# One load instead of two for the gate/up weights of each expert, begun after the second half of the products

## The chip, the cores and the metric

The kernel runs on one core of a Trainium2 chip. The metric is the device time of one execution in microseconds (us). The kernel before takes 1398.07 us, the median of three runs (1396.43, 1398.07 and 1402.14 us).

## What is computed

One transformer layer in float32 for 512 tokens of width 1024: a mixer of four kinds of attention, a layer norm, then a mixture of experts and a second layer norm. The change lies in the mixture of experts alone:

```python
def swiglu(x, w_gate, w_up, w_down):
    return (jax.nn.silu(x @ w_gate) * (x @ w_up)) @ w_down

def step(acc, blk):                      # a block of up to 128 tokens of one expert
    tok, w, e = blk
    yb = swiglu(x_pad[tok], w_gate_e[e], w_up_e[e], w_down_e[e]).astype(jnp.float32) * w[:, None]
    return acc.at[tok].add(yb), None
```

There are 64 experts (and a shared one). The gate and up matrices of an expert are 1024x256 each, together 2 MB; its down matrix is 256x1024, 1 MB. Each token goes to 8 experts.

## The kernel before, in words

The attention part ends some 560 us after the start. The router and the shared expert follow, and the loop over the 64 experts, one block of 128 rows each, runs from about 684 to 1330 us. This loop is what the change touches.

The weights of an expert come in three transfers of 1 MB, all issued by SyncE (queue SP): `load_first` (L537) and `load_second` (L540) bring the two halves of the gate/up weights, 8 KB a partition each, and `load_down` (L543) the down weights. They land in `raw[b]`, b = e % 2, so there are two buffers. ScalarE copies each third into `w_hi_e` with reduced mantissa (L1109), and VectorE writes the rest, raw minus high, into `w_lo_e` (L1426). `w_lo_e[b]` lies at the same addresses as `raw[b]`: a piece of the buffer is free for the next load only when TensorE has finished the products that read the low part.

TensorE works through expert e in this order, called A, turn, B and D below:

- A(e): `gate_up(e, 0)`, 12 products of the first half (L838 high x high, L841 high x low, L844 low x high), which then increments `gu_a`;
- turn: `turn_h(e-1)` (L856) and `turn_slots(e+1)` (L910), transposes;
- B(e): `gate_up(e, 1)`, the same lines for the second half, which increments `gu_b`;
- D(e-1): `down(e-1)`, 12 products (L891), which increments `y_done`.

SP issues the first half of expert e when A(e-2) is done, the second half when B(e-2) is done, and the down weights of e-1 when D(e-3) is done. The four shared tiles count in the same semaphores, hence the `e + QT - 1` of the waits.

ScalarE handles its instructions strictly in this order for expert e: copy out the result of e-2 (`out_y`, L1141), `high_first(e+1)`, `copy_hT(e-1)` (L1127), `high_x(e+1)` (L1133), `high_second(e+1)`, the silu of e (L1123), `high_down(e)`. So `copy_hT(e-1)`, which D(e-1) needs, stands behind `high_first(e+1)`, which waits for the first half of the weights of e+1. VectorE follows with `low_down(e-1)`, the low part of hT (L1447), `low_first(e+1)`, the low part of x (L1452), `make_h(e)` (L1441) and `low_second(e+1)`. GpSimd scatters the results (L1642) and gathers the rows (L1637) with indirect DMAs in a queue of its own, q0; all of SP's transfers are in q1.

Of the kernel before, what the change touches and what calls it, by code (L numbers as in the profile page):

```python
# [37 lines left out]
QT = SEQ // P  # L38
# [20 lines left out]
GU = KT * 2 * F  # L59
# [121 lines left out]
def build(nc, a, out):  # L181
# [9 lines left out]
    with ctx:  # L191
# [3 lines left out]
        def sem(name):  # L195
            return ctx.enter_context(nc.semaphore(name))
# [104 lines left out]
        raw, w_lo_e, w_hi_e = [None, None], [None, None], [None, None]  # L301
# [110 lines left out]
        p0_in = [sem(f"p0_in{b}") for b in range(2)]  # L412
        p1_in = [sem(f"p1_in{b}") for b in range(2)]
        dn_in = [sem(f"dn_in{b}") for b in range(2)]
        p0_hi = sem("p0_hi")
        p1_hi = sem("p1_hi")
# [10 lines left out]
        gu_a = sem("gu_a")  # L427
# [31 lines left out]
        def _(sp):  # L459
# [70 lines left out]
            PART = GU // 2  # L530
# [2 lines left out]
            sp.dma_start(raw[1][:, PART:GU], a["w_gu_s"][:, PART:GU]).then_inc(p1_in[1], 16)  # L533
            sp.dma_start(down_of(raw[1]), a["w_down_s"][0].rearrange("(t p) n -> p t n", p=P)).then_inc(dn_in[1], 16)

            def load_first(e):
                sp.dma_start(raw[e % 2][:, 0:PART], a["w_gu"][e][:, 0:PART]).then_inc(p0_in[e % 2], 16)  # L537

            def load_second(e):
                sp.dma_start(raw[e % 2][:, PART:GU], a["w_gu"][e][:, PART:GU]).then_inc(p1_in[e % 2], 16)  # L540

            def load_down(e):
                sp.dma_start(down_of(raw[e % 2]), a["w_down_e"][0, e].rearrange("(t p) n -> p t n", p=P))\  # L543
                    .then_inc(dn_in[e % 2], 16)
# [5 lines left out]
            store_x1(0)  # L550
            store_x1(1)
            sp.wait_ge(mix_done, QT)
            load_first(0)
            load_second(0)
            load_down(0)
            store_x1(2)
            store_x1(3)
            sp.dma_start(ln[:, 0, :], bass.AP(a["ln2_g"].tensor, 0, [[0, P], [1, D]])).then_inc(ln2_in, 16)
            sp.dma_start(ln[:, 1, :], bass.AP(a["ln2_b"].tensor, 0, [[0, P], [1, D]])).then_inc(ln2_in, 16)
            for e in range(1, N_EXP):  # L560
                sp.wait_ge(gu_a, e + QT - 1)
                load_first(e)
                sp.wait_ge(gu_b, e + QT - 1)
                load_second(e)
                if e >= 2:
                    sp.wait_ge(y_done, e + QT - 2)
                    load_down(e - 1)
# [36 lines left out]
        def _(pe):  # L604
# [14 lines left out]
            def v_of(s, kt):  # L619
                br, h, _, _ = STEPS[s]  # L620
                if br == BR_B:
                    return V[:, kt, V_AT[br, 0], HD * (h // 2):HD * (h // 2) + HD]
                return V[:, kt, V_AT[br, h // 2], HD * (h % 2):HD * (h % 2) + HD]
# [55 lines left out]
            for kind, n in order:  # L679
                if kind == "proj":  # L680
# [5 lines left out]
                    if n == 0:  # L686
                        forget_gates()
                        distance_bias()
                elif kind == "scores":
                    br, h, _, qt = STEPS[n]  # L690
                    if qt == 0:

# [12 lines left out]
                elif kind == "turn":  # L705
                    u = turn_at[kind, n]
                    br, _, _, qt = STEPS[n]
                    pe.wait_ge(probs_made, n + 1)
                    if u >= 2:
# [294 lines left out]
        def _(act):  # L1004
# [99 lines left out]
            PART = GU // 2  # L1104

            def high(e, lo, hi, landed, made):
                b = e % 2
                act.wait_ge(landed[b], 16 * (e // 2 + 1 + b))
                nc.scalar.activation(w_hi_e[b][:, lo:hi], raw[b][:, lo:hi], ACT.Copy).then_inc(made, 1)  # L1109
# [2 lines left out]
                high(e, 0, PART, p0_in, p0_hi)  # L1112

            def high_second(e):
                high(e, PART, GU, p1_in, p1_hi)

            def high_down(e):
                high(e, GU, GU + DN, dn_in, dn_hi)
# [28 lines left out]
            copy_hT(0)  # L1147
            make_silu(1)
            high_second(0)
            copy_hT(1)  # L1150
            make_silu(2)
# [4 lines left out]
            for e in range(N_EXP):  # L1156
                if e >= 2:
                    out_y(e - 2)
                if e + 1 < N_EXP:
                    high_first(e + 1)  # L1160
                if e >= 1:
                    copy_hT(e + QT - 1)
                if e + 1 < N_EXP:
                    high_x(e + 1)
                    high_second(e + 1)
                make_silu(e + QT)
                high_down(e)
# [562 lines left out]
```

## Time and profile before

| | us |
|---|---|
| median of three runs | 1398.07 |
| the profiled execution | 1402.14 |
| its span, first to last instruction | 1400.4 |
| TensorE busy | 1307.5 (93%) |
| VectorE busy | 900.2 (64%) |
| ScalarE busy | 706.9 (50%) |
| GpSimd busy | 420.8 (30%) |

The shares are means over stages of different kinds. Matmuls are pipelined, so the busy time of TensorE counts overlapping instructions once, and waits inside a pipelined stretch can be hidden in it. For a change in the expert loop only the stretch from 684 to 1330 us matters. The time from the issue of a transfer to its landing is called its latency below.

### The profile page before, as it was taken

How to read it: one execution, taken by the hardware profiler on the slowest of the kernel's cores; microseconds unless marked ns; L12 is line 12 of the kernel's file. 1: busy time of each engine (PE TensorE's matmuls, PEld its weight loads, DVE VectorE, ACT ScalarE, POOL GpSimd, SP SyncE). 2: the span in 40 equal slices, each digit the busy share in tenths (PEclk: the TensorE clock that was granted, in tenths of full speed). 3: DMA queues.
4: the chain of work that ended last, by engine and by line, in shares of the span. 5: the costliest groups of instructions: out<-in, count | busy, mean ns of one | idle time of the engine just before them, and what ended most of it. 6: DMA issues, size and time to landing. Idle time of an engine off the chain costs nothing.

```text
span 1400.4 us, 15961 instructions
## 1 busy us (share of the span) xinstructions
PE 1307.5 (93%) x6084; PEld 973.2 (69%) x6084; DVE 900.2 (64%) x1167; ACT 706.9 (50%) x863; POOL 420.8 (30%) x266
## 2 busy tenths in 40 slices
PE   7999999999979999989799999999999999999865
PEld 4989886666656776455587777777777777777722
DVE  4001116645666565564388888888888888888858
ACT  4222333333323221012377888887888778887610
POOL 3232312212223342017233333323233333233204
PEclk9999999999999999989999999999999999999978
DMA  4732202111112151430499999999999999999684
GB/s 154 259 102 72 68 20 68 64 39 38 57 38 67 65 203 54 195 132 19 155 387 373 372 365 370 374 366 370 362 373 360 361 365 371 361 363 349 233 368 179
DMA packets 75291, 311.36 MB, mean 222 GB/s; under 512 B 17660, under 2 KB 17788, under 8 KB 57040
## 3 DMA queue, kind: packets, MB, share of 16 engines
q1 hardware_dynamic: 55728, 276.64, 53.8%
q0 software_dynamic: 19488, 33.70, 6.4%
q8 instruction: 50, 0.82, 0.2%
q14 instruction: 25, 0.20, 0.0%
HBM read 305.74 MB, written 42.01 MB: 248 GB/s over the span
## 4 chain that ended last, share of the span: by engine, by line
PE 65%; DMA 21%; DVE 4%; ACT 4%; issue 3%; POOL 3%; POOLq 0%; SPq 0%; DVEq 0%; ACTq 0%
DMA raw<-in_w_gu 19%; PE PS L647 18%; PE PS L891 9%; PE PS L841 5%; PE PS L844 4%; PE PS L838 4%; PE PS L755 4%; PE PS L703 4%; PE PS L773 3%; ACT w_hi_e L1109 3%; PE PS L726 3%; POOL tab_d L1628 2%; PE PS L714 2%; PE PS L675 2%; PE PS L676 2%
## 5 line engine op out<-in xcount | busy, mean ns | idle before, releaser
L1426 DVE TENSOR_TENSOR w_lo_e<-raw,w_hi_e 128x2048 fp32r<-128x2048 f32 x192 | 435.3, 2285 | 14.3 <-ACT w_hi_e L1109 14.0
L1109 ACT ACTIVATE w_hi_e<-raw 128x2048 fp32r<-128x2048 f32 x192 | 368.3, 1919 | 119.8 <-DMA raw<-in_w_gu 75.1
L1642 POOL DMA_INDIRECT y_d<-y_slots,tab x64 | 120.8, 1887 | 412.1 <-ACT y_slots L1141 284.7
L1596 POOL TENSOR_TENSOR w_lo<-ring,w_hi 128x1024 fp32r<-128x1024 f32 x54 | 128.3, 2376 | 327.0 <-ACT w_hi L1016 327.0
L1269 DVE CUSTOM_DVE_ANT_0 region<-PS,region 128x128 f32<-128x128 f32 (+1 forms) x64 | 30.6, 478 | 183.2 <-PE PS L703 181.1
L838 PE MATMUL PS<-w_hi_e,xs_hi 128*128 128x512 f32 x512 | 144.2, 403 | 0.0
L841 PE MATMUL PS<-w_hi_e,xs_lo 128*128 128x512 f32 x512 | 142.8, 401 | 0.0
L844 PE MATMUL PS<-w_lo_e,xs_hi 128*128 128x512 f32 x512 | 137.5, 390 | 0.0
L1060 ACT ACTIVATE region<-region,nmax 128x128 f32<-128x128 f32 (+3 forms) x80 | 43.6, 546 | 150.3 <-DVE nmax L1269 150.0
L841 PEld LDWEIGHTS PS<-w_hi_e,xs_lo 128*128 128x128 f32 x512 | 92.7, 188 | 30.6 <-DVE xs_lo L1452 12.4
L844 PEld LDWEIGHTS PS<-w_lo_e,xs_hi 128*128 128x128 f32 x512 | 96.2, 188 | 20.8
L838 PEld LDWEIGHTS PS<-w_hi_e,xs_hi 128*128 128x128 f32 x512 | 91.9, 189 | 16.1 <-issue 0.5
L647 PE MATMUL PS<-x_hi,w_hi 128*128 128x512 f32 x368 | 101.0, 418 | 0.0
L891 PE MATMUL PS<-w_hi_e,hT_hi 128*128 128x512 f32 x256 | 73.4, 408 | 26.2 <-ACT hT_hi L1127 26.0
L1637 POOL DMA_INDIRECT x_slots<-x_d,tab x64 | 84.8, 1324 | 39.2 <-issue 18.3
L647 PE MATMUL PS<-x_hi,w_lo 128*128 128x512 f32 x376 | 95.5, 396 | 0.0
L647 PE MATMUL PS<-x_lo,w_hi 128*128 128x512 f32 x368 | 91.9, 392 | 0.0
L1452 DVE TENSOR_TENSOR xs_lo<-PS,xs_hi 128x1024 fp32r<-128x1024 f32 x64 | 78.0, 1218 | 10.3 <-ACT xs_hi L1133 10.3
L647 PEld LDWEIGHTS PS<-x_hi,w_hi 128*128 128x128 f32 x368 | 68.2, 193 | 16.7 <-issue 4.1
L891 PEld LDWEIGHTS PS<-w_hi_e,hT_hi 128*128 128x128 f32 x256 | 44.8, 188 | 48.7 <-ACT hT_hi L1127 41.4
L647 PEld LDWEIGHTS PS<-x_hi,w_lo 128*128 128x128 f32 x376 | 69.0, 188 | 13.6
L647 PEld LDWEIGHTS PS<-x_lo,w_hi 128*128 128x128 f32 x368 | 68.5, 188 | 14.2
(182 smaller groups left out, 2154.3 us busy)
## 6 DMA issues: line engine op xcount, KB each, us to landing
raw<-in_w_gu SPq DMA_DIRECT2D x128, 1024.0 KB, 11.3
raw<-in_w_down_e SPq DMA_DIRECT2D x64, 1024.0 KB, 11.0
ring<-in_w_merge SPq DMA_DIRECT2D x32, 640.0 KB, 4.0
parts<-y_d SPq DMA_DIRECT2D x8, 1536.0 KB, 16.2
ring<-in_w_proj SPq DMA_DIRECT2D x22, 512.0 KB, 3.7
region<-in_w_out SPq DMA_DIRECT2D x1, 4096.0 KB, 14.1
parts<-y_d SPq DMA_DIRECT2D x4, 1024.0 KB, 19.9
bias_d<-bias_rows SPq DMA_DIRECT2D x3, 1280.0 KB, 11.7
```

Of the source, the lines that this page charges most:

```text
L647: mm = nc.tensor.matmul(PS[:, bank, :], (w_hi, w_hi, w_lo)[i][:, n % HALVES, c, :], (x_hi, x_lo, x_hi)[i][:, c, :], start=(i == 0 and c == 0),
L703: nc.tensor.matmul(PS[:, S_BANK + n % 2, 0:nk * P], q, k, start=True, stop=True)\
L838: nc.tensor.matmul(to, xs_hi[:, b, c, :], wh[:, c, :], start=(c == 0), stop=False)
L841: nc.tensor.matmul(to, xs_lo[:, b, c, :], wh[:, c, :], start=False, stop=False)
L844: mm = nc.tensor.matmul(to, xs_hi[:, b, c, :], wl[:, c, :], start=False, stop=(c == KT - 1))
L891: mm = nc.tensor.matmul(PS[:, Y_BANK + n, :], hx[:, s % 2, half, :], w[:, half, n * 512:(n + 1) * 512], start=(first and half == 0), stop= ...
L1109: nc.scalar.activation(w_hi_e[b][:, lo:hi], raw[b][:, lo:hi], ACT.Copy).then_inc(made, 1)
L1426: nc.vector.tensor_tensor(w_lo_e[b][:, lo:hi], raw[b][:, lo:hi], w_hi_e[b][:, lo:hi].bitcast(F32), ALU.subtract).then_inc(made, 1)
L1452: nc.vector.tensor_tensor(xs_lo[:, e % 2, :, :], PS[:, X_BANK:X_BANK + 2, :].rearrange("p a (c n) -> p (a c) n", n=P), xs_hi[:, e % 2, :, ...
L1596: nc.gpsimd.tensor_tensor(wl, w, wh.bitcast(F32), ALU.subtract).then_inc(w_lo_made, 1)
L1637: pool.indirect_dma_start(x_slots[:, b, :], None, x1_d, bass.IndirectOffsetOnAxis(ap=rows, axis=0), bounds_check=last_tok, oob_is_err=Fals ...
L1642: pool.indirect_dma_start(y_d, bass.IndirectOffsetOnAxis(ap=rows, axis=0), y_slots[:, b, :], None, bounds_check=last_row, oob_is_err=False ...
```

## The change

The two functions `load_first` and `load_second` go. One transfer of 2 MB, 16 KB a partition, takes their place; it is issued where `load_second` was, after the wait for `gu_b`. The wait for `gu_a` in front of `load_first` goes too. Both ScalarE copies of the gate/up weights now wait on the semaphore of the one transfer, `p0_in`. The order of the instructions on all compute engines stays, and so does the place of `load_down`.

```diff
-            def load_first(e):
-                sp.dma_start(raw[e % 2][:, 0:PART], a["w_gu"][e][:, 0:PART]).then_inc(p0_in[e % 2], 16)
-
-            def load_second(e):
-                sp.dma_start(raw[e % 2][:, PART:GU], a["w_gu"][e][:, PART:GU]).then_inc(p1_in[e % 2], 16)
-
@@
             sp.wait_ge(mix_done, QT)
-            load_first(0)
-            load_second(0)
+            sp.dma_start(raw[0][:, 0:GU], a["w_gu"][0]).then_inc(p0_in[0], 16)
             load_down(0)
@@
             for e in range(1, N_EXP):
-                sp.wait_ge(gu_a, e + QT - 1)
-                load_first(e)
                 sp.wait_ge(gu_b, e + QT - 1)
-                load_second(e)
+                sp.dma_start(raw[e % 2][:, 0:GU], a["w_gu"][e]).then_inc(p0_in[e % 2], 16)
                 if e >= 2:
                     sp.wait_ge(y_done, e + QT - 2)
                     load_down(e - 1)
@@
             def high_second(e):
-                high(e, PART, GU, p1_in, p1_hi)
+                high(e, PART, GU, p0_in, p1_hi)
```

## Rows read from the trace of the kernel before

**Rows 1.** The page: DMA share and rate in 40 slices of 35 us.

```profile
DMA  4732202111112151430499999999999999999684
GB/s 154 259 102 72 68 20 68 64 39 38 57 38 67 65 203 54 195 132 19 155 387 373 372 365 370 374 366 370 362 373 360 361 365 371 361 363 349 233 368 179
```

**Rows 2.** Busy time by stretch: us, each engine's busy (instructions), PEclk, DMA share, GB/s.

```profile
726.00:1298.00 572.00, 548.46 (x2626) 441.02 (x2625) 487.60 (x343) 459.11 (x400) 183.21 (x114) 1.00 0.98 366
```

**Rows 3.** The chain that ended last, in order of time: start, us, what.

```profile
1024.62 12.26 DMA raw<-in_w_gu
1036.88 0.02 issue
1036.90 1.92 ACT w_hi_e L1109
1038.82 0.28 ACT hT_hi L1127
1039.09 0.04 issue
1039.13 3.01 PE PS L891 x12
1042.15 0.91 PE PS L838 x4
1043.05 1.07 PE PS L841 x4
1044.12 0.92 PE PS L844 x4
1045.05 0.22 PE PS L856 x2
1045.26 0.89 PE PS L910 x8
1046.15 0.93 PE PS L838 x4
...
1048.00 0.91 PE PS L844 x4
1048.91 2.72 PE PS L891 x12
```

**Rows 4.** SP's loads, 720 to 1330 us: L537, then L540 (instructions, latency).

```profile
L537 SPq DMA_DIRECT2D raw<-in_w_gu x58: 327/328/328, 726.8 to 1298.4; - x58
DMA to landing us min/median/max: 9.6/12.0/13.4
...
L540 SPq DMA_DIRECT2D raw<-in_w_gu x59: 327/328/328, 721.4 to 1302.2; - x59
DMA to landing us min/median/max: 9.6/11.2/12.3
```

**Rows 5.** Queues, 700 to 1300 us: packets, MB, share of the 16 engines.

```profile
q1 hardware_dynamic: 33663, 188.99, 84.5%
q0 software_dynamic: 17114, 30.99, 13.5%
```

**Rows 6.** Expert 0's loads, issued together: L537, then L540, with their latency.

```profile
L537 SPq DMA_DIRECT2D raw<-in_w_gu x1: 333/333/333, 616.6 to 616.6; - x1
DMA to landing us min/median/max: 4.9/4.9/4.9
...
L540 SPq DMA_DIRECT2D raw<-in_w_gu x1: 433/433/433, 617.0 to 617.0; - x1
DMA to landing us min/median/max: 7.1/7.1/7.1
```

**Rows 7.** Timeline of SP's queue in the first experts: start, us, instruction.

```profile
692.00 0.33 SPq L537 DMA_DIRECT2D raw<-in_w_gu  x1
695.63 0.33 SPq L540 DMA_DIRECT2D raw<-in_w_gu  x1
...
702.20 0.33 SPq L540 DMA_DIRECT2D raw<-in_w_gu  x1
...
711.50 0.33 SPq L540 DMA_DIRECT2D raw<-in_w_gu  x1
```

**Rows 8.** The chain, from the last experts: start, us, what.

```profile
1306.65 0.91 PE PS L838 x4
...
1313.37 2.72 PE PS L891 x12
1316.09 0.91 PE PS L838 x4
```

**Rows 9.** DMA, 1345 to 1362 us (loads with rows of 12 and 8 KB).

```profile
DMA packets 728, 7.30 MB, mean 430 GB/s; under 512 B 80, under 2 KB 80, under 8 KB 80
q1 hardware_dynamic: 728, 7.30, 101.4%
```

## Prediction

> **What bounds the kernel now.** I read the page's slices first. From the slice at 700 us to the one at 1295 us the DMA engines are at nine tenths or more and move 349 to 387 GB/s [rows 1]; no other stage looks like this. The stretch view of that stage says the same: DMA share 0.98, 366 GB/s, and TensorE busy for 548.46 of 572 us, VectorE for 487.60, ScalarE for 459.11, with TensorE's clock granted in full, 2.4 GHz [rows 2]. Nothing has much slack, so I went to the chain of waits to see which wait ends last. It repeats: a first-half load of 12.26 us, ScalarE's high part of 1.92, its copy of hT, then D on TensorE and work without a gap until another load is issued [rows 3]. The copy of hT waits for nothing of its own there. It stands behind `high_first` in ScalarE's order, and that stands and waits for the weights. So D(k-1) starts, at the earliest, 1.92 + 0.28 + 0.04 + 0.02 = 2.25 us after the first half of expert k+1 has landed.
>
> How long is a turn? The first-half loads go out at 726.8 to 1298.4 us, 58 of them [rows 4]: 571.6 / 57 = 10.03 us per expert. TensorE alone, never waiting, needs 1316.09 - 1306.65 = 9.44 us for A, turn, B and D [rows 8]. A 1 MB load takes 12.0 us (first half) or 11.2 us (second) from issue to landing in the loop [rows 4] and 4.9 us where the queue is empty [rows 6]; so some 6 to 7 us of each is queueing behind other loads. The kernel is near three limits at once: the DMA engines, TensorE, and the loop of buffer, load and ScalarE.
>
> **The change part by part.**
>
> (1) Two issues of 0.33 us become one, and a wait on `gu_a` goes. SP does nothing else, and its issues lie beside TensorE's work. Worth nothing by itself. SP is held at no new place: the wait for `gu_b` was there already, `load_down` behind it keeps its place, and the GpSimd queue isn't touched.
>
> (2) The first half is requested later. From the end of A(k) to the end of B(k) TensorE does turn and B: 1048.91 - 1045.05 = 3.86 us [rows 3]. Every first half sets out 3.86 us later in a turn.
>
> (3) The first half also becomes usable later, with the last byte of 2 MB. Expert 0's two halves were issued back to back, at 616.6 and 617.0 us, with the queue otherwise empty. The first was there 4.9 us after its issue, the second at 617.0 + 7.1 = 624.1, that is 7.5 us after the first issue [rows 6]. That is the nearest row to one empty-queue load of 2 MB: 7.5 us, against 4.9 for half of it.
>
> (4) The second half isn't late: it's issued where it was, and ScalarE takes it after `high_first`, `copy_hT` and `high_x`. `high_second` finds it landed, always. This gains nothing, since ScalarE is behind `high_first`.
>
> (5) The sum is a loop over two experts, since there are two buffers. Call L the time from the issue of the 2 MB to its landing. The load for k+1 is issued at the end of B(k-1), lands L later, D(k-1) starts 2.25 us after that, and from the start of D(k-1) to the end of B(k+1) TensorE needs 1048.91 - 1039.13 = 9.78 us [rows 3]. The end of B(k+1) issues the load for k+3. So two turns last at least L + 2.25 + 9.78 + 0.02 = L + 12.05 us. TensorE's own limit is 2 x 9.44 = 18.9, which would want L at 6.8 us or less, below even the empty-queue 7.5. Today's two turns are 20.06 us, which is matched at L = 8.0.
>
> (6) What is L inside the loop? The trace doesn't hold such a load; two bounds. Below: 7.5 us, with nothing in between. Above: today each megabyte takes a third of a turn, 3.34 us, where in the empty queue the second followed the first by 7.5 - 4.9 = 2.6 us; 0.74 us more for each of two megabytes gives 7.5 + 1.5 = 9.0. Between them lies the share of the gathers and scatters: q0 takes 13.5% of the engines' time against 84.5% for q1 [rows 5], which stretches the 5.2 us of moving 2 MB by 13.5/84.5, 0.8 us, to L = 8.3. The landing is that of the slowest of 16 engines, so I go above that mean and take 8.65, the middle of 8.3 and 9.0. Does other q1 traffic lie ahead of it? The down load goes out 3 us after the 2 MB and follows it; 3 MB of q1 at 3.34 us each is 10.0 us, less than the new turn of 10.35 us. The queue is just about empty when the next 2 MB comes, so no queueing is added. It is close, though: 1 us of it is the upper end of my range.
>
> Two turns are then 8.65 + 12.05 = 20.70 us, 10.35 a turn.
>
> (7) Start and end. B(0) ended at 695.63 and B(1) at 702.20 [rows 7]; neither hangs on a changed load, since expert 1's waits only for the shared tiles. The load for expert 2 goes out at 695.63 instead of 692.00, lands at 703.15 with L = 7.5, D(0) starts at 705.4 and B(2) ends at 715.2 instead of 711.50: +3.7. From there every second B is 20.70 us after the last: B(62) ends at 715.2 + 30 x 20.70 = 1336.2 us. Before, it ended at 1313.37 us [rows 8]. The rest of the kernel (D(61), expert 63, the weighted sum) hangs on it by the same steps as before. The sum is +22.8 us.
>
> The profiled execution took 1402.14 us with a span of 1400.4; it would take 1425. It was the slowest of three runs, 4.1 above the median, so against the median of 1398.07 I say 1421 us. Each 0.1 us in L is 3 us in the end.
>
> The Trainium skill's page DMA: Bandwidth & Descriptors, section Rules for kernel authors, has a rule on each side. One asks to issue a DMA early and wait on its semaphore late, which the change gives up for half the weights; the 3.86 us above are what that costs here. The other asks for 1 MiB or more a DMA, and the same page's fit (2.0 us plus bytes over 436 GB/s) would make L 6.8 us for 2 MB, by which two turns would be TensorE's 18.9 and the kernel some 31 us faster. Against the fit stands the pair of loads above, which took 7.5, and 4.9 where the fit says 4.4.
>
> **The rivals.**
>
> Faster: the DMA engines are the bound and the larger transfer unloads them. For it: share 0.98 at 366 GB/s [rows 2], while the final loads with 12 and 8 KB rows reach 430 GB/s [rows 9], so the same engines can do a sixth more when less is mixed; one transfer start of three goes. If the queue then empties so far that L is its empty-queue 7.5, two turns are 19.55, B(62) ends at 715.2 + 30 x 19.55 = 1301.7, and the time is 1386 us, 12 less. Were L short enough for TensorE's 18.88 to set two turns, B(62) would end at 715.2 + 30 x 18.88 = 1281.6, and the time would be 1366 us; the fit of the page DMA: Bandwidth & Descriptors (the Trainium skill, as above) leads there. Against it: the gathers and scatters are still there in q0 whatever q1 does, and the smaller load of the engines is worth something only through L.
>
> Same: the delay is absorbed. Today 6 to 7 us of each latency are queueing, so a load that sets out 3.86 us later may lose only its place in a queue, and the engines' throughput, which would be as before, sets the turn. It holds if L is 8.0, between my two lower values; the time is then 1398 + 3.7 - 0.3, 1401 us. For it: 3 MB at the present rate and the turn of 10.03 agree. Against it: it needs an L in a narrow band (7.7 to 8.1).
>
> Much slower: the queue isn't empty when the 2 MB are issued. If the down load before it is late by 1 us, L is 9.65, two turns 21.7, and B(62) ends at 1366: 1451 us. It decides from the point where 3 MB of q1 take longer than a turn. Against it: each turn that gets longer empties the queue again.
>
> That the change doesn't do what it says isn't likely: rows of 12 KB run at 430 GB/s [rows 9], and both copies read from the one buffer that the load fills.
>
> **How the numbers follow.** One measurement of this kernel can tell about 0.5%, 7 us, from no change. That is L above 8.1 for slower, below 7.65 for faster. Forecast (L 8.1 to 9.6): 0.60. Much slower: 0.07. Same: 0.18. Faster with L about 7.5: 0.12; with TensorE as the limit: 0.03. So slower 0.67, same 0.18, faster 0.15. The range runs from 1390 (L 7.6) to 1450 (L 9.6); it leaves out the better half of the faster case and most of the much slower one.
>
> **What would show it.** The chain should have a 2 MB load in every second expert's turn, followed by ScalarE's high part, the copy of hT and D, with 9.8 us of TensorE before the next issue; today it has one in three. Its latency should be about 8.65 us median, and well under today's 12.0. The issues should be 10.35 us apart; `high_first` should wait in nearly every turn and `high_second` never; the DMA share should fall to 0.95 or less, and TensorE's wait at L891 for hT grow. The down loads should land faster than today's. I'm wrong if the share stays at 0.98 with a shorter turn (then the engines were the bound), if D starts right behind B (then the loop isn't closed by ScalarE), or if L isn't near 8.65.

## The result: 1497.7 us, 7.0% slower

The changed kernel takes 1497.73 us, the median of four runs (1496.07 to 1500.12); the ratio to the kernel before is 1.0699, with an interval of 1.0676 to 1.0722. I had forecast slower, and 1421 us with a range to 1450. The direction was right; the size was four times what I gave it.

The page of the changed kernel, which answers to [rows 1], then its stretch view (columns as in [rows 2]):

```profile
DMA  5721201111112524306888888888879888888684
GB/s 174 256 77 56 68 28 62 53 39 51 53 54 70 191 78 155 141 3 234 306 312 335 308 317 320 317 314 327 318 296 341 303 327 321 304 328 330 236 334 186
```

```profile
740.00:1380.00 640.00, 561.74 (x2556) 448.49 (x2556) 472.63 (x335) 440.91 (x392) 212.46 (x111) 0.95 0.87 319
```

TensorE, VectorE, ScalarE and the DMA engines are all less busy in the loop than before (GpSimd is at a third in both): the DMA share is 0.87 at 319 GB/s, where it was 0.98 at 366. So nothing is used up; something waits. The mean clock that TensorE was granted is 0.95 there: part of the stretch was at 1.2 GHz, where the mean was 1.00 (2.4 GHz) before. The chain that ended last (start, us, what) says what waits, and the line of the loads gives their latency ([rows 3] and [rows 4] before):

```profile
1015.50 10.44 DMA raw<-in_w_gu
1025.94 0.02 issue
1025.96 1.91 ACT w_hi_e L1100
1027.88 0.28 ACT hT_hi L1118
1028.15 0.04 issue
1028.20 3.02 PE PS L882 x12
1031.22 0.91 PE PS L829 x4
...
1037.06 0.92 PE PS L835 x4
1037.98 0.02 issue
1037.99 11.13 DMA raw<-in_w_gu
```

```profile
L555 SPq DMA_DIRECT2D raw<-in_w_gu x58: 327/328/328, 740.0 to 1395.8; - x58
DMA to landing us min/median/max: 8.2/10.8/11.6
```

From issue to issue of the same buffer this cycle is 1037.99 - 1015.50 = 22.49 us, which is 10.44 + 12.05: the loop that the prediction wrote down, to the hundredth. What is off is first of all the 10.44. The median of the landings that the profile lists is 10.8; over 55 loads of the loop, from the issue to the start of the ScalarE copy that waits for them, the mean is 10.4. The prediction had 8.65. The issues are (1395.8 - 740.0) / 57 = 11.5 us apart, not 10.35.

ScalarE's high part waited for gate/up weights in every turn, and never for the down weights (columns: us in total, times, longest):

```profile
ACT w_hi_e L1100 <- DMA raw<-in_w_gu: 205.9, 58, 5.7
```

### The profile page after: what moved, and what is told of

Same layout as the page of the kernel before. It is cut to its first block, busy times and chain, and to the rows that moved or that the text cites. A ratio compares the mean times of both kernels' runs of the same rounds, so it can differ in the third digit from the quotient of the medians.

```text
span 1496.7 us, 15897 instructions
## 1 busy us (share of the span) xinstructions
PE 1336.7 (89%) x6084; PEld 993.9 (66%) x6084; DVE 896.6 (60%) x1167; ACT 697.5 (47%) x863; POOL 456.0 (30%) x266
## 4 chain that ended last, share of the span: by engine, by line
PE 66%; DMA 21%; DVE 5%; ACT 4%; issue 2%; another core or an unknown queue 0%; POOL 0%; POOLq 0%; SPq 0%; DVEq 0%; ACTq 0%
DMA raw<-in_w_gu 20%; PE PS L638 17%; PE PS L882 9%; PE PS L832 5%; PE PS L829 4%; PE PS L835 4%; ACT w_hi_e L1100 4%; PE PS L746 3%; PE PS L694 3%; PE PS L764 3%; PE PS L717 2%; PE PS L901 2%; PE PS L705 2%; PE PS L667 2%; PE PS L665 2%
## 5 line engine op out<-in xcount | busy, mean ns | idle before, releaser
L1633 POOL DMA_INDIRECT y_d<-y_slots,tab x64 | 171.7, 2682 | 469.3 <-ACT y_slots L1132 458.1
L882 PE MATMUL PS<-w_hi_e,hT_hi 128*128 128x512 f32 x256 | 83.7, 453 | 91.2 <-ACT hT_hi L1118 91.2
L1438 DVE TENSOR_TENSOR hT_lo<-PS,hT_hi 128x256 fp32r<-128x256 f32 x64 | 27.1, 424 | 189.3 <-ACT hT_hi L1118 186.8
L882 PEld LDWEIGHTS PS<-w_hi_e,hT_hi 128*128 128x128 f32 x256 | 48.4, 205 | 118.8 <-ACT hT_hi L1118 111.1
L638 PE MATMUL PS<-x_hi,w_lo 128*128 128x512 f32 x376 | 95.4, 396 | 0.0
L1628 POOL DMA_INDIRECT x_slots<-x_d,tab x64 | 69.9, 1092 | 44.4 <-PE PS L901 24.7
L882 PE MATMUL PS<-w_lo_e,hT_hi 128*128 128x512 f32 x256 | 82.6, 452 | 0.0
## 6 DMA issues: line engine op xcount, KB each, us to landing
raw<-in_w_gu SPq DMA_DIRECT2D x64, 2048.0 KB, 10.8
bias_d<-bias_rows SPq DMA_DIRECT2D x3, 1280.0 KB, 11.5
```

The lines of the kernel that those rows point to most:

```text
L638: mm = nc.tensor.matmul(PS[:, bank, :], (w_hi, w_hi, w_lo)[i][:, n % HALVES, c, :], (x_hi, x_lo, x_hi)[i][:, c, :], start=(i == 0 and c == 0),
L882: mm = nc.tensor.matmul(PS[:, Y_BANK + n, :], hx[:, s % 2, half, :], w[:, half, n * 512:(n + 1) * 512], start=(first and half == 0), stop= ...
L1628: pool.indirect_dma_start(x_slots[:, b, :], None, x1_d, bass.IndirectOffsetOnAxis(ap=rows, axis=0), bounds_check=last_tok, oob_is_err=Fals ...
L1633: pool.indirect_dma_start(y_d, bass.IndirectOffsetOnAxis(ap=rows, axis=0), y_slots[:, b, :], None, bounds_check=last_row, oob_is_err=False ...
```

## The experiments

L is the time from the end of B to the landing of what ScalarE's `high_first` waits for, and R the rest of the loop up to the issue of the next load of the same buffer, so that two turns are L + R. In the changed kernel R is 12.05 in the cycle above and 12.04 in the median, but 12.6 in the mean: in 23 of 56 cycles it is longer. The turns are those of the loads of one line between 740 and 1300 us, last issue minus first over their number less one.

| kernel | us | ratio to before, interval | turn | L |
|---|---|---|---|---|
| changed | 1497.7 | 1.070 (1.068 to 1.072) | 11.5 | 10.4 |
| e1 | 1410.7 | 1.0065 (1.0043 to 1.0087) | 10.09 | 8.1 |
| e2 | 1418.2 | 1.012 (1.009 to 1.014) | 10.26 | 8.4 |
| e3 | 1490.1 | 1.064 (1.062 to 1.066) | 11.40 | 10.3 |
| e4 | 1454.7 | 1.038 (1.032 to 1.044) | 10.77 | 9.3 |
| e5 | 1422.8 | 1.015 (1.010 to 1.020) | 10.23 | 8.2 |
| e6 | 1495.5 | 1.068 (1.065 to 1.071) | 11.45 | 10.6 |
| e7 | 1358.5 | 0.971 (0.968 to 0.974) | 9.33 | |
| e8 | 1357.8 | 0.970 (0.967 to 0.973) | 9.31 | |
| e9 | 1480.3 | 1.057 (1.052 to 1.062) | 11.18 | |
| e10 | 1439.9 | 1.029 (1.023 to 1.036) | 10.52 | |
| e11 | 1405.3 | 1.003 (1.000 to 1.007) | 10.08 | |
| e12 | 1409.1 | 1.007 (1.005 to 1.010) | 10.07 | 10.7 |
| e13 | 1388.1 | 0.993 (0.990 to 0.995) | 9.64 | 9.7 |

L is a mean over 49 to 56 loads of the loop, taken to the start of the ScalarE copy that waits for them, some 0.02 us after the landing.

### The change taken apart: e1, e2, e3

e1: loads as before, but `high_first` waits for both.

```diff
             def high_first(e):
+                act.wait_ge(p1_in[e % 2], 16 * (e // 2 + 1 + e % 2))
                 high(e, 0, PART, p0_in, p0_hi)
```

> The kernel before, first halves issued as early as ever, but ScalarE takes the first half only when both halves of 1 MB have landed. Theory 1 (the time is lost because ScalarE waits for the last byte of a load that sets out at the end of B; two turns last L + 12.05 us with L from the end of B to the whole landing, and size and number of transfers don't matter): today's second halves take 11.2 us, so two turns are near 23 us and the time near that of the changed kernel, 1480 to 1510 us. Theory 2 (a 2 MB transfer of 16 KB rows is itself slow to land beside the gathers): this kernel has none, so it stays near 1421 us or below. Theory 3 (the late issue of the first half costs it): nothing is late here, 1400 us.

1410.7 us, 0.65% slower. Theory 1 fell in its number: I had put in the 11.2 us that second halves took before. But this latency didn't belong to the load alone. With the wait for the whole, the second half lands 8.0 us after its issue, and not 11.2 [rows 4]:

```profile
L540 SPq DMA_DIRECT2D raw<-in_w_gu x56: 327/328/328, 747.6 to 1302.0; - x56
  ACT w_hi_e L1109: 124.0, 56
DMA to landing us min/median/max: 7.3/8.0/9.5
```

When it was issued, 0.9 MB of earlier loads of q1 were left in the mean, in place of 1.2 (counted by the packets of the two traces). Two turns are 8.1 + 12.05 = 20.15 us, a turn of 10.1, as measured.

e2: both halves issued at the end of B, each with its own semaphore. e3: the same, and `high_first` waits for both, as in e1.

```diff
-                sp.wait_ge(gu_a, e + QT - 1)
-                load_first(e)
                 sp.wait_ge(gu_b, e + QT - 1)
+                load_first(e)
                 load_second(e)
```

> The kernel before with both 1 MB halves issued back to back at the end of B, each with its own semaphore; ScalarE takes the first half when that has landed. Theory 1 (what counts is when the first half is usable): the first half lands some 2.6 to 3.3 us before the second, L is 10.8 - 3 = 7.8, two turns are 19.9 us, the time is about 1400 us. Theory 3 (the later issue costs it all): like the changed kernel, 1490 us. Theory 2 (the 2 MB transfer is slow): about 1400 us too.

> As before, both 1 MB halves issued back to back at the end of B, and ScalarE takes the first half only when both have landed: the changed kernel in all but the size of the transfers and their rows (8 KB in place of 16 KB). Theory 1: equal to the changed kernel within 1%, 1485 to 1510 us. Theory 2 (the 2 MB transfer is slow by itself): L about 8.65 and 1421 us.

e2 gives 1418.2 us, e3 1490.1 us. So the late issue alone costs 1.2%, the wait for the whole alone 0.65%, and both together 6.4%. Each alone leaves one megabyte between the end of B and the landing, with L at 8.1 to 8.4; together it's two megabytes, with L at 10.3. The 2 MB transfer with rows of 16 KB adds another half a percent (1.064 against 1.070, intervals apart), with 0.1 us more in L. Theory 1 holds for the change as a whole, and theory 2, a 2 MB transfer slow by itself, is out as the cause of the loss.

### What makes the 2 MB take 10.4 us: e4, e5

> The changed kernel, with the rows of an expert's block dealt alternately to partitions 0 to 63 and 64 to 127, where they fill the block from partition 0 up in both kernels (64 of 128 on the average are live). The result is the same. Theory A (L is 10.8 and not 8.65 because gathers and scatters load the DMA engines of the low partitions alone, and a load lands when the slowest of 16 engines is done): L falls to about 9 and the time to 1420 to 1450 us. Theory B (L is long from the volume of q0, or from the down load ahead in q1): nothing changes, 1497 us.

```diff
-            pool.dma_start(tab[:, :, :], tab_rows[0]).then_inc(tab_in, 16)
+            alternate = tab_rows[0].rearrange("(q h) e b -> h q e b", h=2)
+            for h in range(2):
+                pool.dma_start(tab[h * 64:(h + 1) * 64, :, :], alternate[h]).then_inc(tab_in, 16)
...
-            pool.wait_ge(tab_in, 16)
+            pool.wait_ge(tab_in, 32)
```

1454.7 us, 43 us less, and L is 9.3: the direction of theory A, a little above its range. In e5 most of the bytes of the rows go (256 B for 4 KB), with all waits kept; for experts 4 to 59 it leaves out most of each row.

```diff
+            def gather_few(rows, b, done):
+                pool.sem_inc(gathers_begun, 1)
+                pool.indirect_dma_start(x_slots[:, b, 0:64], None, x1_d.rearrange("s (g w) -> (s g) w", w=64), ...
...
-                    gather(tab[:, j, 0:1], j % 2, slots_in[j % 2])
+                    (gather if j < 4 or j >= 60 else gather_few)(tab[:, j, 0:1], j % 2, slots_in[j % 2])
```

> The changed kernel; for experts 4 to 59 the gathers and scatters move rows of 64 elements (256 B) instead of 1024 (4 KB), from and to other places, and the final sum reads other data in place of the results, so all the waits and instructions stay and the bytes of q0 go. Theory A with its volume (q0's bytes are what makes L 10.4 instead of the empty queue's 7.9): L falls to 8.0 to 8.5, two turns to 20 to 20.6 us, the time to 1400 to 1425 us. Theory B (the down load ahead in q1, or the start of a load beside others, makes it long): L stays above 9.3 and the time above 1450 us.

1422.8 us, L 8.2. The queues of e5 between 740 and 1310 us, which answer to [rows 5], and the latency of the loads (issues by line: count, KB, median us to landing):

```profile
q1 hardware_dynamic: 23077, 175.33, 82.8%
q0 software_dynamic: 4034, 3.05, 1.8%
...
raw<-in_w_gu SPq DMA_DIRECT2D x55, 2048.0 KB, 8.0
raw<-in_w_down_e SPq DMA_DIRECT2D x56, 1024.0 KB, 7.6
```

In an empty queue the changed kernel's first 2 MB load took 7.9 us:

```profile
L547 SPq DMA_DIRECT2D raw<-in_w_gu x1: 333/333/333, 615.2 to 615.2; - x1
DMA to landing us min/median/max: 7.9/7.9/7.9
```

So of the 10.4 us some 7.9 are the load itself, 2.2 (10.4 - 8.2) go with the bytes of gathers and scatters, and half of these (10.4 - 9.3) go when the same bytes are dealt to both halves of the partitions.

What e5 doesn't settle is the way in which these bytes act. They can slow the 2 MB themselves, or the down load in front of it in q1. That load was the last thing issued before the 2 MB, as in this stretch of the changed kernel's SP queue:

```profile
1170.00 0.38 SPq L537 DMA_DIRECT2D raw<-in_w_down_e  x1
1176.59 0.33 SPq L555 DMA_DIRECT2D raw<-in_w_gu  x1
```

6.6 us are less than the 7.6 that a down load takes even in e5. I counted the packets of q1 in the trace of the changed kernel, for 54 of its loads: at 15 issues nothing was left of earlier loads, and L was 9.0 us in the mean; at the other 39 some 0.2 MB was left (0.5 at most), and L was 11.0. In e5 something was left at 28 of 54 issues, and L was 8.0 there and 8.3 at the others. So a remainder goes with a long L only where the rows' bytes are there too. No run takes the down load away and leaves the rows, so how the 2.2 us divide between the two stays open.

### TensorE's clock: e6

```diff
+                    pe.wait_ge(dn_hi, e)
+                    for _ in range(6):
+                        nc.tensor.matmul(PS[:, 5, :], xs_hi[:, e % 2, 0, :],
+                                         down_of(w_hi_e[(e - 1) % 2])[:, 0, 0:512], start=True, stop=True)
                     down(e - 1)
```

> The changed kernel, with six products more on TensorE between B(e) and D(e-1), into a PSUM bank that nobody reads. TensorE does them in the time in which it would wait for hT (some 1.4 us of them), so the loop over L doesn't get longer. Theory C (part of the loss is TensorE's clock, granted at 1.2 instead of 2.4 GHz in 61 us of the loop after its longer waits): the low stretches all but go and the time falls by 15 to 30 us, to 1468 to 1483 us. Rival (the low clock lies in waits and costs nothing): 1497 us or more.

```profile
740.00:1380.00 640.00, 613.12 (x2910) 496.22 (x2909) 474.43 (x336) 442.23 (x392) 215.68 (x113) 1.00 0.87 321
```

The mean clock is 1.00 in place of 0.95 (2.4 GHz in all but one short stretch), TensorE is busier, and the time is 1495.5 us: the interval of the ratio overlaps with the changed kernel's. Theory C's 15 to 30 us didn't come. In the means R fell from 12.6 to 12.3 us and L rose from 10.4 to 10.6.

This doesn't price the low clock by itself, for the six products have a price too. In some turns hT is ready at once, and then they stand in the chain (L942), in front of D:

```profile
1199.87 0.91 PE PS L835 x4
1200.77 1.36 PE PS L942 x6
1202.13 2.72 PE PS L882 x12
```

What the run shows is that keeping the clock up in this way gives nothing that can be measured.

### The kernel before, with the rows dealt: e7, e8, e11

e7 has the edit of e4 in the kernel before.

> The kernel before, with the live rows dealt to both halves of the partitions as in the changed kernel's variant. Theory A (gathers and scatters load the engines of the low partitions alone, and these set the turn of 10.03 us): the turn falls towards TensorE's 9.44 us, 9.5 to 9.75, and the time to 1365 to 1385 us. Theory B (all 16 engines are equally full): nothing changes, 1398 us.

1358.5 us, 2.9% faster than the kernel before, a little below what was expected. The gate/up loads of 1 MB land in 8.3 us in the median; before it was 11.3.

```profile
740.00:1280.00 540.00, 538.98 (x2661) 452.30 (x2660) 491.23 (x348) 469.71 (x406) 222.67 (x113) 1.00 0.99 389
```

TensorE is busy without a gap, and the turn is its own 9.33 us. The DMA share is 0.99, what it was before, and the rate 389 instead of 366 GB/s [rows 2]. The Trainium skill (DMA: Bandwidth & Descriptors, section The descriptor swizzle) says that in a transfer to 128 partitions eight of the 16 engines write partitions 0 to 63 and the other eight the rest; the gains of e4 and e7 fit this, but no run shows a single engine's load.

```diff
-                if e + 1 < N_EXP:
-                    high_first(e + 1)
                 if e >= 1:
                     copy_hT(e + QT - 1)
+                if e + 1 < N_EXP:
+                    high_first(e + 1)
```

> The kernel before with the rows dealt to both halves and ScalarE's copy of hT ahead of the high part of the first half. If D's wait behind the weights is what is left above TensorE's 9.44 us, the turn is 9.44 to 9.55 and the time 1360 to 1372 us, below the variant with the rows alone. Rival (the high part now waits for turn, which comes only after A): the same as that variant or up to 10 us slower.

> The kernel before with the copy of hT first, rows as they were. If its turn of 10.03 us is set by the DMA engines of the low partitions and not by D's wait, little changes: 1388 to 1400 us. If D's wait behind the weights sets it, the turn falls to 9.4 and the time to 1360 us.

With this edit too, e8 takes 1357.8 us: the same as e7, since TensorE has no wait left to lose. e11, the edit alone in the kernel before, takes 1405.3, no gain. D's wait behind the weights was there [rows 3], but removing it gives nothing while the rows lie as they did; dealing the rows alone brings the turn down to TensorE's own.

### The other side of the loop: e9, e10, e12, e13

e9 is the changed kernel with the copy of hT first, e10 the same with dealt rows.

> The changed kernel with ScalarE's copy of hT ahead of the high part of the first half, so that D no longer stands behind the weights. If the loop is closed by ScalarE's order (two turns = L + 12.05 us), it becomes landing, high part 1.94, low part 2.3, last third of A, turn, B: two turns at least L + 9.05, 19.5 us with L at 10.4; the fuller queue may lengthen L, so the turn is 9.8 to 10.2 us and the time 1385 to 1415 us. Rival (the order doesn't matter, since A needs the weights right after D): above 1450 us.

> The changed kernel with the copy of hT first and the rows dealt to both halves of the partitions. Two turns at least L + 9.05 = 18.4 us with L at 9.4, so TensorE's own turn of 9.33 us sets the pace: 1358 to 1372 us, equal within 1% to the kernel before with dealt rows, and the change costs nothing. Rival (one load of 2 MB is worse at any order): 1380 us or more.

1480.3 and 1439.9 us: 17 and 15 us less than without the edit, where I expected some 90. My R of 9.05 was wrong, and e9's chain shows why.

```profile
1009.24 10.94 DMA raw<-in_w_gu
...
1020.20 1.93 ACT w_hi_e L1100
...
1022.15 2.29 DVE w_lo_e L1417
1024.44 1.15 DVE xs_lo L1443
...
1025.64 1.19 PE PS L832 x4
...
1031.64 10.99 DMA raw<-in_w_gu
```

D no longer waits, but A does: VectorE makes the low part of x behind the low part of the weights, and A's second group of products needs it. R is 22.40 - 10.94 = 11.46, only 0.6 less. In e12 x goes ahead of the weights on both engines; e13 is e12 with dealt rows.

```diff
-                if e + 1 < N_EXP:
-                    high_first(e + 1)
                 if e >= 1:
                     copy_hT(e + QT - 1)
                 if e + 1 < N_EXP:
                     high_x(e + 1)
+                    high_first(e + 1)
                     high_second(e + 1)
@@
-                    low_first(e + 1)
                     low_x(e + 1)
+                    low_first(e + 1)
```

> The changed kernel with both copies that TensorE's turn and D need (hT, and x high and low) ahead of the weights of the first half, on ScalarE and VectorE. With the copy of hT alone moved, the chain was landing, ScalarE 1.93, VectorE 2.29 for the low part of the weights, 1.15 for that of x, then TensorE 5.98 to the next issue: two turns = L + 11.4. Without the 1.15 us and with x ready, it is L + 1.94 + 2.31 + 0.92 + 1.11 + 2.75 = L + 9.05. With L at 10.4 to 11 two turns are 19.5 to 20.1 us: 1385 to 1410 us. Rival (once a 2 MB load is ahead, the DMA engines of the low partitions lengthen L by what the order gives back): 1440 us or more.

> The same, with the rows dealt to both halves of the partitions. L at 9.4 to 10 us gives 18.5 to 19.1 us for two turns against TensorE's 18.7: the turn 9.35 to 9.6 us, 1358 to 1378 us, within 1.5% of the kernel before with dealt rows. Rival (one 2 MB load is slower at any order): 1390 us or more.

```profile
1017.23 10.89 DMA raw<-in_w_gu
...
1028.14 1.93 ACT w_hi_e L1100
...
1030.09 2.30 DVE w_lo_e L1416
...
1032.44 1.21 PE PS L835 x4
...
1037.54 10.75 DMA raw<-in_w_gu
```

Two turns are 1037.54 - 1017.23 = 20.31 us in e12, L 10.89 and R 9.42, and the kernel takes 1409.1 us. This is the telling run: the same 2 MB load, issued as late and landing no sooner (L 10.7), costs 0.7% instead of 7.0%. The rival of e12 falls. e13 has a turn of 9.64 and 1388.1 us, above the 1378 expected and above e7: two turns are 19.3 us (L 9.7, R 9.6 in the means), still more than TensorE's 18.7, and its ScalarE still waits for the load in every turn. One late load is worse than two early ones with dealt rows (1388 against 1358.5 us), though no longer by much. No run has e12's order in the kernel before.

## Why the prediction was wrong, point by point

Steps (1), (2) and (4) held: nothing points to SP's work, and `high_second` never waited.

Step (3), the empty-queue load: 7.9 us, not 7.5. Small.

Step (5), the loop: right. The cycle in the trace is L + 12.05, and e1, e2 and e5 have turns of 10.09, 10.26 and 10.23 us where (L + 12.05) / 2 gives 10.1, 10.2 and 10.1. At the longest L it is short by more: (10.4 + 12.05) / 2 = 11.2 against 11.5. In 16 of 56 cycles D takes 4.3 us or more instead of 3.0, and in each of them the clock was granted at 1.2 GHz for 3.4 us or more while D ran. Here is such a D near the end of the loop, and the stretch view of its time (0.50 is 1.2 GHz):

```profile
1397.60 4.61 PE PS L882 x12
```

```profile
1398.10:1401.50 3.40, 3.40 (x9) 2.64 (x9) 3.40 (x3) 3.40 (x4) 0.00 (x0) 0.50 0.96 412
```

Step (6), L inside the loop, is the one that failed: 10.4 for 8.65, and above even the upper bound of 9.0. I spread q0's share over 16 engines and over the whole turn and got 0.8 us, where e5 puts it at 2.2 and e4 shows that half of this lies in the way the rows are dealt. I also wrote that the queue is just about empty when the next 2 MB comes. It was at 15 of 54 issues, and there L was 9.0; at the others, with 0.2 MB left in the mean, it was 11.0. The down load goes out 4.8 us after the 2 MB in the mean, not 3, which leaves it less time before the next. And the upper bound, 0.74 us for each megabyte, was taken from a kernel in which TensorE's own pace and a full queue set the spacing of landings; it was a throughput, and I used it as the price of one load that everything waits for. I had written down that the slowest engine sets the landing, and added 0.35 us for it.

The sum, by the end of B(62): 1408.82 in the changed kernel against 1313.37 before [rows 8], +95.4 us. Of these I had 22.8. The start was 3.4 later than my 715.2 (B(2) ended at 718.60; its load took 9.86 and its D 5.49 us). From there 30 pairs of turns took 690.2 us, 23.01 each, not 20.70: 69.2 us. Of the 2.3 us a pair, 1.8 are L, and 0.5 are R, which the formula held at 12.05: the long Ds at the low clock, and turns in which TensorE, late from the turn before, came to D after hT was ready. My sum put this second term at nothing.

The rivals: "faster" had the DMA engines as the bound. They were not full in the sense of that rival, and yet something in them did set the pace before: e7 gained 2.9% by dealing the rows to both halves. "Same" needed L at 8.0. "Much slower" came nearest, though at 1451 us it too was short by 47. Its condition, a queue that isn't empty when the 2 MB are issued, held at most issues; how much of L that made is open, as said under e5. The fit of the Trainium skill's page DMA: Bandwidth & Descriptors (section Anatomy of one DMA — SWDGE (gpsimd) path), which the prediction used for an L of 6.8 us, is given there for transfers that GpSimd issues. Expert 0's load of 2 MB, issued by SyncE, took 7.9.

What would show it: the waits, the shares and the gap of 9.8 us came as I wrote; the latency and the spacing did not. The trace of the changed kernel doesn't list when its down loads landed. The low clock was a term that I had not thought of. As an estimate, 16 Ds of some 1.6 us more are 26 us; each of them is in one of two loops that run side by side, so about half, some 13 us, reaches the end. e6 was 2 us faster than the changed kernel, with the price of its own products in it, so no run confirms the estimate.

## What to carry to other kernels

Write the loop of buffer, load and dependent engines as L + R before sizing anything: the change lost 7% with R at 12 us and more and 0.7% with R at 9.4, with the same late load. Size L beside whatever else runs on the DMA engines, and by how unevenly that may load them, and don't take an average rate or a latency from another schedule: a gate/up load of 1 MB took 4.9 us in the empty queue, and the second half took 11.2 in the loop before and 8.0 in e1, where one more wait was all that had changed. Look at how gathers and scatters with part of their rows live are spread over the partitions: dealing them to both halves took a few lines, and brought the kernel from 1398 to 1358.5 us.

## What the runs showed of the hardware

A DMA share of 0.98 did not mean that the DMA engines could do no more: with the rows dealt to both halves the share was 0.99 and the rate 389 instead of 366 GB/s. The share adds up the times that packets took, and it seems that these hold waits; no run shows which.

TensorE was granted 1.2 GHz in part of the loop of the changed kernel (0.95 in the mean), in which it waits for hT again and again. With six idle products in these waits the mean was 1.00; one stretch of 3.4 us at 1.2 GHz was left (1043.7 to 1047.1 us).
